# The modulation of a two-layer transformer block with its weight tiles turned: VectorE sums each row, and four slabs share the first block of inputs

## The reference, cut to what matters

```python
c_act = jax.nn.silu(c)
mod = c_act @ w_ada[l] + b_ada[l]          # w_ada[l] is 2048 x 12288
shift_a, scale_a, gate_a, shift_m, scale_m, gate_m = jnp.split(mod, 6)
h = rms_norm(x, g_pre_mix[l]) * (1.0 + scale_a) + shift_a
y = token_mixer(h, ...)                    # h @ w_in, mLSTM and attention, @ w_out
x = x + gate_a * rms_norm(y, g_post_mix[l])
h = rms_norm(x, g_pre_mlp[l]) * (1.0 + scale_m) + shift_m
y = squared_relu_mlp(h, w_up[l], w_down[l])
x = x + gate_m * rms_norm(y, g_post_mlp[l])
```

## Time and profile before

| what | value |
|---|---|
| median of 3 runs | 3728.34 us (3727.72 to 3730.37) |
| the profiled execution's own time | 3729.29 us |
| its span | 3727.5 us |
| PE busy | 3394.7 us, 91% |
| DVE busy | 2639.3 us, 71% |
| ACT busy | 1569.2 us, 42% |
| mean granted TensorE clock | 0.929 of full |

### The profile page before, as it was taken

How to read it: one execution, slowest core, us unless ns; L and a number is a source line. 1 busy time by engine, 2 the same in 40 slices (tenths; PEclk the granted TensorE clock), 3 DMA queues, 4 the chain that set the end, 5 groups by cost and what they waited for, 6 DMA issues and landing times.

```text
span 3727.5 us, 46843 instructions
## 1 busy us (share of the span) xinstructions
PE 3394.7 (91%) x18574; PEld 2861.8 (77%) x18574; DVE 2639.3 (71%) x4213; ACT 1569.2 (42%) x2160; POOL 0.2 (0%) x4
## 2 busy tenths in 40 slices
PE   1888889999999988889889999998988999899997
PEld 1676777888888867778678888886877588688886
DVE  7878777777777778777776655567499665656665
ACT  1444554343434454444434444445333054534343
POOL 0000000000000000000000000000000000000000
PEclk6788899999999988989899999998859999899999
DMA  9756576777777745456466555554405045354353
GB/s 397 290 212 226 218 267 223 273 259 275 256 279 257 268 168 223 178 192 254 182 238 236 186 188 191 191 186 158 177 28 200 13 166 207 125 190 151 123 181 113
DMA packets 111304, 759.09 MB, mean 204 GB/s; under 512 B 13936, under 2 KB 18288, under 8 KB 21104
## 3 DMA queue, kind: packets, MB, share of 16 engines
q1 hardware_dynamic: 107936, 749.72, 55.5%
q10 hardware_dynamic: 3152, 6.38, 0.5%
HBM read 747.58 MB, written 8.39 MB: 203 GB/s over the span
## 4 chain that ended last, share of the span: by engine, by line
PE 65%; DVE 21%; ACT 7%; issue 3%; ACTq 0%; DMA 0%; DVEq 0%; SPq 0%
PE bk L301 64%; DVE wl L1196 7%; ACT wh L691 5%; DVE acc L1204 4%; DVE sq L1204 2%; DVE pr L1196 1%; ACT L691 1%; DVE X L1196 1%; PE bk L305 1%; DVE ss L1196 1%; DVE Hst L1196 1%; DVE hb L1196 1%; DVE HX L1204 1%; DVE sm L1380 0%; DVE co L1204 0%
## 5 line engine op out<-in xcount | busy, mean ns | idle before, releaser
L1196 DVE TENSOR_TENSOR wl<-raw,wh 128x2048 fp32r<-128x2048 f32 x507 | 1161.2, 2290 | 439.7 <-ACT wh L691 439.0
L301 PE MATMUL bk<-HX,wh 128*128 128x512 f32 x5040 | 1288.6, 406 | 59.8 <-ACT HX L691 32.0
L301 PEld LDWEIGHTS bk<-HX,wh 128*128 128x128 f32 x5040 | 952.8, 194 | 301.6 <-issue 67.9
L691 ACT ACTIVATE wh<-raw 128x2048 fp32r<-128x2048 f32 x507 | 966.9, 1907 | 72.5 <-DMA raw<-in_w_in 72.4
L301 PEld LDWEIGHTS bk<-HX,wl 128*128 128x128 f32 x5040 | 654.0, 194 | 34.8 <-DVE wl L1196 10.9
L301 PE MATMUL bk<-HX,wl 128*128 128x256 f32 x5040 | 662.3, 285 | 6.9 <-DVE wl L1196 6.8
L301 PE MATMUL bk<-hb,wh 128*128 128x512 f32 x2048 | 495.0, 393 | 15.1 <-ACT hb L691 6.0
L301 PEld LDWEIGHTS bk<-hb,wh 128*128 128x128 f32 x2048 | 378.1, 189 | 96.6 <-issue 13.4
L1204 DVE SCALAR_TENSOR_TENSOR acc<-raw,sm,acc 128x2048 f32<-128x2048 f32 x180 | 423.2, 2351 | 21.2 <-DMA raw<-in_w_ada 1.1
L301 PEld LDWEIGHTS bk<-hb,wl 128*128 128x128 f32 x2048 | 266.1, 194 | 9.8
L301 PE MATMUL bk<-hb,wl 128*128 128x256 f32 x2048 | 269.5, 285 | 0.0
(11 more groups left out here) (259 smaller groups left out, 2914.5 us busy)
## 6 DMA issues: line engine op xcount, KB each, us to landing
raw<-in_w_ada SPq DMA_DIRECT2D x192, 1024.0 KB, 4.9
raw<-in_w_up SPq DMA_DIRECT2D x128, 1024.0 KB, 4.8
raw<-in_w_down SPq DMA_DIRECT2D x128, 1024.0 KB, 4.8
raw<-in_w_in SPq DMA_DIRECT2D x74, 1024.0 KB, 4.9
raw<-in_kv_w SPq DMA_DIRECT2D x33, 1024.0 KB, 4.8
raw<-in_w_out SPq DMA_DIRECT2D x32, 1024.0 KB, 5.3
raw<-in_s_w_in SPq DMA_DIRECT2D x32, 1024.0 KB, 4.9
raw<-in_fox_w_in SPq DMA_DIRECT2D x32, 1024.0 KB, 4.8
```

Source lines behind the costliest of these rows:

```text
L301: return e.matmul(o_, l_, r_, start=start, stop=stop, skip_group_check=True)
L691: return e.activation(o_, i_, f, **kw)
L1196: return e.tensor_tensor(o_, a_, b_, op)
```

## The change

The modulation's tiles are stored the other way round: 128 outputs on the partitions and all 2048 inputs along the row. `CB` holds silu(c), twice as large, the same in every partition; it is made once from a new 1 MB input `c_row` by a Tanh on ACT and one operation of DVE. One scalar_tensor_tensor per tile then multiplies the tile by CB and by 0.5, writes the product back over the tile in RAW, and its accumulator writes the row sums: 128 finished outputs, one column of `MOD`. `ACC`, `ROW`, PE's sums, ACT's row copies, the 40 small DMAs, and the wait of each tile for the one before are gone.

The two first pieces come in turns, tile k of the scale and tile k of the shift, and every four pairs are finished into four blocks of h. Slabs 0 to 3 are loaded and split between these tiles, into WH and WL places of their own (1 to 4) and banks 0 to 3. `ramp` multiplies them side by side, block by block of h, and starts when all four are split. The constants (`cst`) are loaded behind the first five tiles instead of first. The other 160 tiles are spread anew: behind slabs 4 to 51, one each; 80 behind MLP0's slabs (64 before); 16 behind the last slab of IN1 and the first 15 of OUT1 (32 in IN1 and OUT1 before, 25 of them in IN1); 16 in MLP1.

```diff
-def spread(first, last):
-    return [first + (last - first) * i // 15 for i in range(16)]
-AFTER = ([[-1] * 16, [-1] * 16]
-         + [spread(0, 13), spread(16, 31), spread(34, 47)]
-         + [spread(J_MLP[0] + 32 * p, J_MLP[0] + 32 * p + 28) for p in range(4)]
-         + [spread(J_IN[1] + 3, J_IN[1] + 22), spread(J_IN[1] + 25, J_IN[1] + 46)]
-         + [spread(J_MLP[1] + 2, J_MLP[1] + 30)])
-SUM_AFTER = {14: 2, 32: 3, 49: 4, J_IN[1] + 23: 9, J_IN[1] + 48: 10, J_MLP[1] + 32: 11}
-SUM_AFTER.update({J_MLP[0] + 32 * p + 30: 5 + p for p in range(4)})
+RAMP = 4
+def spread(first, last, n):
+    return [first + (last - first) * i // (n - 1) for i in range(n)]
+AFTER = (spread(4, 51, 48) + spread(J_MLP[0], J_MLP[0] + 124, 80) + spread(J_OUT[1] - 1, J_OUT[1] + 14, 16)
+         + spread(J_MLP[1] + 2, J_MLP[1] + 32, 16))
...
+for _k in range(16):
+    _tile_next(_k)
+    _tile_next(16 + _k)
+    if _k % 3 == 2 and _k // 3 < RAMP:
+        _slab_next(_k // 3)
+for _j in range(RAMP, N_SLABS):
+    _slab_next(_j)
...
+BANK_OF = [j if j < RAMP else j % 3 for j in range(N_SLABS)]
+PLACE_OF = [j + 1 if j < RAMP else j % 2 for j in range(N_SLABS)]
...
                 return first
-            def sums(j):
-                if j not in SUM_AFTER:
-                    return
-                p = SUM_AFTER[j]
-                e.wait_ge(s_free, TILE_POS[16 * p + 15] + 1)
-                bank = claim(3)
-                for c in range(4):
-                    last = mm(bank[32 * c:32 * c + 1, :], ONES[:, 0:1], ACC[:, 512 * c:512 * c + 512], True, True)
-                last.then_inc(s_sum, 1)
-                release[3] = (s_sumr, p - 1)
+            def ramp(j0, count, x, first):
+                e.wait_ge(s_hi, j0 + count)
+                e.wait_ge(s_free, POS[j0 + count - 1] + 1)
+                banks = [claim(BANK_OF[j0 + r]) for r in range(count)]
+                for k in range(KT):
+                    first(k)
+                    for r in range(count):
+                        w = PLACE_OF[j0 + r]
+                        mm(banks[r][:, :], WH[w][:, k, :], x(k).rearrange("p a t -> p (a t)"), k == 0, False)
+                        last = mm(banks[r][:, 0:T], WL[w][:, k, :], x(k)[:, 0, :], False, k == KT - 1)
+                last.then_inc(s_slab, count)
+                release[3] = (s_ev, j0 + count)
             def x_sum(i):
...
             def layer(l):
+                if l == 0:
+                    ramp(0, RAMP, hx, h_ready(0))
                 for n in range(N_IN):
-                    slab(J_IN[l] + n, hx, None if n else h_ready(2 * l))
+                    if l or n >= RAMP:
+                        slab(J_IN[l] + n, hx, None if n else h_ready(2 * l))
...
-            for p in range(2):
-                bank = claim(4 + p)
-                e.wait_ge(s_free, TILE_POS[16 * p + 15] + 1)
-                for k in range(KT):
-                    last = mm(bank[:, k:k + 1], ACC[:, k::16], ONES[:, 0:1], True, True)
-                last.then_inc(s_sum, 1)
-                release[4 + p] = (s_mod, p + 1)
...
-                if j >= 2:
-                    e.wait_ge(s_slab, j - 1)
-                act(WH[j % 2][:, :, :], RAW[POS[j] % RING][:, :, :], ACT.Copy).then_inc(s_hi, 1)
+                if before(j, PLACE_OF) >= 0:
+                    e.wait_ge(s_slab, before(j, PLACE_OF) + 1)
+                act(WH[PLACE_OF[j]][:, :, :], RAW[POS[j] % RING][:, :, :], ACT.Copy).then_inc(s_hi, 1)
...
-            def sums(j):
-                if j - 1 not in SUM_AFTER:
-                    return
-                p = SUM_AFTER[j - 1]
-                l, piece = PIECES[p]
-                e.wait_ge(s_sum, p + 1)
-                if p > 2:
-                    e.wait_ge(s_row, 64 * (p - 2))
-                for c in range(4):
-                    last = act(ROW[32 * c:32 * c + 1, :], BK[3][32 * c:32 * c + 1, :], ACT.Copy)
-                last.then_inc(s_sumr, 1)
-                e.wait_ge(s_sumr, p - 1)
-                for c in range(4):
-                    e.dma_start(MOD[32 * c:32 * c + 32, 6 * l + piece, :],
-                                ROW[32 * c:32 * c + 1, :].rearrange("o (p k) -> o p k", k=16)).then_inc(s_row, 16)
...
             def layer(l):
-                for n in range(N_IN):
-                    if n:
+                for n in range(0 if l else RAMP, N_IN):
+                    if l == 0 and n == RAMP:
+                        for i in range(RAMP):
+                            mixer_half(l, i)
...
             e.wait_ge(s_x, 16)
+            e.wait_ge(s_cb0, 1)
             x_rms(0)
-            high(0)
-            for l in range(2):
-                to_h(2 * l, MOD[:, 6 * l + SHIFT_A, :])
-                layer(l)
+            for k in range(KT):
+                if k % 4 == 0:
+                    for j in ((0,), (1,), (2, 3), ())[k // 4]:
+                        high(j)
+                to_h_block(0, k, MOD[:, SHIFT_A, :])
...
-                ada(j)
-            def ada(j):
-                for t in TILES_AFTER.get(j, []):
-                    p, k = divmod(t, 16)
-                    place = TILE_POS[t]
-                    raw = RAW[place % RING][:, :, :].rearrange("p a b -> p (a b)")
-                    e.wait_ge(s_raw[place % RING], 16 * (place // RING + 1))
-                    if k == 0:
-                        if p:
-                            e.wait_ge(s_sum, p)
-                        ts(ACC[:, :], raw, CA[:, 0:1], None, ALU.mult).then_inc(s_free, 1)
-                    else:
-                        e.wait_ge(s_free, place)
-                        stt(ACC[:, :], raw, CA[:, k:k + 1], ACC[:, :], ALU.mult, ALU.add).then_inc(s_free, 1)
...
+                if j >= RAMP:
+                    for t in TILES_AFTER.get(j, []):
+                        tile(t)
+            def tile(t):
+                p, k = divmod(t, 16)
                 l, piece = PIECES[p]
-                col_ = MOD[:, 6 * l + piece, :]
+                place = TILE_POS[t]
+                raw = RAW[place % RING][:, :, :].rearrange("p a b -> p (a b)")
+                e.wait_ge(s_raw[place % RING], 16 * (place // RING + 1))
+                stt(raw, raw, 0.5, CB[:, :], ALU.mult, ALU.mult, MOD[:, 6 * l + piece, k:k + 1]).then_inc(s_free, 1)
+                if p > 1 and k == 15:
+                    e.wait_ge(s_free, place + 1)
+                    ended(p, slice(0, 16)).then_inc(s_mod, 1)
...
-            def sums(j):
-                if j - 3 in SUM_AFTER:
-                    p = SUM_AFTER[j - 3]
-                    l, piece = PIECES[p]
-                    e.wait_ge(s_row, 64 * (p - 1))
-                    piece_ended(p, MOD[:, 6 * l + piece, :])
...
-            ccol = PRM[:, C_COL:C_COL + 16]
+            e.wait_ge(s_ct0, 1)
+            stt(CB[:, :], SQ[:, 0:8, :].rearrange("p k t -> p (k t)"), 1.0, CB[:, :], ALU.add,
+                ALU.mult).then_inc(s_cb0, 1)
+            e.wait_ge(s_cb0, 1)
             e.wait_ge(s_prm, 16)
-            e.wait_ge(s_ce, 1)
-            settled(ts(CE, CE, 1.0, None, ALU.add))
-            settled(e.reciprocal(CE, CE))
-            tt(CA, CE, ccol, ALU.mult).then_inc(s_ca, 1)
-            e.wait_ge(s_ca, 1)
             e.wait_ge(s_cst, 16)
-            ada(-1)
-            low(0)
-            for p in range(2):
-                e.wait_ge(s_sum, p + 1)
-                piece_ended(p, BK[4 + p][:, 0:16])
-            for l in range(2):
-                gs, sh = modulation(l, SCALE_A), modulation(l, SHIFT_A)
-                to_h(2 * l, gs, sh)
-                layer(l)
+            gs, sh = MOD[:, SCALE_A, :], MOD[:, SHIFT_A, :]
+            for k in range(KT):
+                tile(k)
+                tile(16 + k)
+                if k % 3 == 2 and k // 3 < RAMP:
+                    low(k // 3)
+                if k % 4 == 3:
+                    q = slice(k - 3, k + 1)
+                    e.wait_ge(s_free, TILE_POS[16 + k] + 1)
+                    ended(0, q)
+                    settled(ended(1, q))
+                    if k == 3:
+                        e.wait_ge(s_rx, 1)
+                    for i in range(k - 3, k + 1):
+                        scaled(0, i, gs)
+                    for i in range(k - 3, k + 1):
+                        h_low(0, i, sh)
+            low(RAMP)
+            layer(0)
+            gs, sh = modulation(1, SCALE_A), modulation(1, SHIFT_A)
+            to_h(2, gs, sh)
+            layer(1)
             third()
             fourth()
...
-            e.dma_start(CST[:, :], d["cst"]).then_inc(s_cst, 16)
+            e.dma_start(CB[:, :], d["c_row"]).then_inc(s_c, 16)
             e.dma_start(PRM[:, :], d["prm"]).then_inc(s_prm, 16)
-            for j in range(-1, N_SLABS):
-                others(j)
-                if j >= 0:
-                    load(POS[j], source(j))
-                for t in TILES_AFTER.get(j, []):
-                    (l, piece), k = PIECES[t // 16], t % 16
-                    load(TILE_POS[t], d["w_ada"][l, piece, k])
```

(92 more changed lines are left out.)

52 lines of the change are left out of this document (23 added, 29 removed).

## The result

The changed kernel takes 3669.72 us (median, 3665.61 to 3671.2), the one before 3729.07 beside it (3727.72 to 3730.37): a ratio of 0.9839, interval 0.9822 to 0.9856. So it is faster by 59 us. The forecast was 3695 with a range of 3674 to 3720: the right side, and a time outside the range. The profiled execution of the changed kernel took 3671.2 us, with a span of 3669.4.

The account below looks back on a forecast made before the run. No single bound: PE in MLP stages without tiles, waits between PE and DVE in the mixers, DVE at the start. Terms -7 + 0 - 1 + 4 - 25 - 1 - 3 = -33 gave 3696, predicted 3695 us, range 3674 to 3720.

Parts of the forecast that it names:

- IN1: -25: Stage IN1: 25 tiles leave and one comes in, saving 25 us, the largest term.
- The chain gave 33: IN1's chain of waits: 13 whole tiles, 30.6 us, with the sum's 2.4 make 33, taken to bound the gain.
- the comparison of IN0 and IN1: IN0, with more tiles and sums, took only 4.5 us more than IN1: some 0.5 us a tile, 12 in all.
- The catching up: In IN1, PE idle for 43.5 us and below full clock was said to have room to catch up.
- my second rival: IN1 and start: fewer waits keep PE at full clock; IN1 gives 33, the start 10, total 3683 or so; chance 0.12.
- The tile: 2.36: Every new tile on DVE: 2.351 less 0.09 overlap plus 0.1 for writing out the accumulator; ends 2.26 and 2.46 us.
- The start: -7: Before slab 4: DVE bounds after the constants at 25.7; slab 4 at 136.4 instead of 143.4; ends -10 and +3.
- MLP0: +4: Stage MLP0: three more tiles on the path +7.4, 35 tiles at 0.1 less -3.5; ends -6 and +8.
- MLP1: -3: Stage MLP1: 7 tiles in late up slabs instead of 8 (-2.5), and 7 x 0.1; ends -5 and 0.
- IN0 and the OUT stages: IN0: more tiles offset by cheaper ones and fewer sums, 0; OUT0 and OUT1: tiles free, sums gone, -1 us each.
- The rivals on the slow side: Every tile: writing out the accumulator is dear (chance 0.05, 3750 us), or the tile runs at half speed (0.03, about 3970).
- The halved throughput: Every tile: two non-bf16 sources with row sums run at half throughput, about 4.6 us a tile, about 3970 total; chance 0.03.

Follow-up runs that it names:

- the two last runs in IN1: Two kernels with most MLP tiles in down slabs, plus tiles back in IN1: 14 on its chain of waits, 3646.83 us; 11 off it, 3613.8 us.
- n_pointer: The changed kernel with the factor 0.5 read from a column in SBUF instead of a constant in the instruction: 3674.54 us, run once.
- n_down: The changed kernel with most tiles of MLP0 and MLP1 moved from the up slabs into the down slabs: 3619.89 us, ratio 0.9708.
- n_off_chain: The kernel of n_down with 11 tiles back in IN1, behind slabs where the chain of waits passed no tile: 3613.8 us, run once.
- n_best: n_off_chain with the constants loaded ahead of the first tile instead of behind the fifth: 3606.24 us, ratio 0.9674.
- n_best2: n_best with IN0's 33 tiles moved off that stage's chain of waits, several behind one slab: 3588.29 us, ratio 0.9627.

## Why the prediction was right or wrong

**IN1: -25, measured -34.8; this step failed.** The chain gave 33, and I took 25 because the comparison of IN0 and IN1 made a tile worth 0.5 us, and because idle PE would catch up. The comparison was wrong: it counted tiles, and the two last runs in IN1 show that a count says nothing. There 14 in the wrong places cost 30 us, and 11 in others about one. The catching up was half right. The chain's 13 tiles were 30.6 us, and PE's idle time fell by 21.1 only. What the "bound" left out was the clock: 62 us at half clock became 28, and PE's busy time fell by 11.3 more than the sum's 2.4. That the bound of 33 came so close to 34.8 is therefore partly luck: less of the tiles' time came off than it says, and the clock made up for it. The clock stood in the earlier trace rows at 0.90, and my second rival named this mechanism with 0.12; it came about, though the clock rose to 0.95 and not to full. Its 3683 was still too high, as it had the start at -10 and a tile at 2.36.

**The tile: 2.36, measured 2.21; this term was mis-sized, and its ends too.** The lower end of 2.26 took 2.351 for the instruction. The pointer factor was in the row (`sm` among the sources), but I gave it no price; `n_pointer` puts it at 0.061. The read-out, for which I put 0.1, is not on the path: it overlaps the next instruction. At the start (32 tiles), in MLP0 (35) and in MLP1 (7) 0.15 less is 11 us. Of the 25 us between the sum's -33 and the -58 of the spans, IN1 holds 10, and these three stages hold the other 15.

**The start: -7, measured -12.5.** The steps held: the wait for the constants (25.5 for 25.7), then DVE as the bound. Of the 5.5 us that the forecast was too late, 4.2 are there at the last h already (122.0 for 126.2), and 32 tiles at 0.15 are 4.8. The rest is in the last four blocks, of which only part ran at half clock (6.8 us), and in the step to slab 4. The end of -10 was too near.

**MLP0: +4, measured -2.6; MLP1: -3, measured -5.8.** The three more tiles in MLP0 and the 35 cheaper ones both counted as said; 35 x 0.25 = 8.8 of gain stood against 7, where I had 3.5. MLP1's 7 tiles give 1.8 by the price and the one that left 2.46; 1.5 us I can't place. A full price for every tile fits here because DVE is behind PE with so many of them in the late up slabs. I did not see that it has a floor: `n_down` shows that few enough tiles cost nothing there.

**IN0 and the OUT stages** came as forecast (-0.3, -0.1, -1.2 for 0, -1, -1). That IN0's two more tiles and its cheaper ones cancelled is my reading; no run separates them.

**The rivals on the slow side** fell with the first row of the tile. The halved throughput (the Trainium skill, Vector Engine (DVE) Microarchitecture Reference, Points that are easy to get wrong) does not hold here: two fp32 sources in SBUF with the accumulator written out take 2.284 us, as long as a plain tensor_tensor of the size, 2.29.

**The range** of 3674 to 3720 failed by 4 us. Its lower end allowed the sum 21 us more. The price of a tile enters the start, MLP0 and MLP1 alike, so a cheaper tile makes these stages better at once and their errors (15 us) don't cancel; IN1's 10 us came on top.

## What to carry to other kernels

Price work that is moved off a chain of waits by the pieces of it that the chain passes, not by a stage's total divided by the number of pieces. Their full length came out within 2 us in IN1 (14 tiles at 2.21 are 30.9; measured 29.8 and 30.1), but 12 us of that was PE's slower clock and 18 its idle time, so the clock is not to be added on top. In IN0 the same price for 14 tiles gave 23.2. Before moving filler work out of a stage, try other places within it: the same 33 tiles behind other slabs of IN0 saved 23 us in that stage. In a stage that PE bounds, filler is free up to PE's pace, so spread it thinly, one in three up slabs here, instead of one behind nearly each.

## What the hardware did that was not expected

- DVE's read of its accumulator takes 0.082 us and starts with the instruction behind it, so it adds nothing to the path: tiles follow each other at 2.21.
- A wait for DVE's own instruction before costs 0.19 us (2.40 against 2.21), although that instruction ends only 0.07 behind the point where the next could start.
- A factor read from a column of SBUF in place of a constant costs 0.06 us in a 128x2048 fp32 scalar_tensor_tensor (2.345 against 2.284).
- DVE's tiles in the wrong slabs slow TensorE beyond the waits: the same matmuls of IN1 took 252 us at a mean clock of 0.90 and 240 at 0.95.
- The clock also moved the stage with every tile of it in place: IN1 took 259.1 us at 0.96 in `n_off_chain` and in `n_best`, and 264.0 at 0.94 in `n_best2`, with 23.6 to 23.7 us of idle PE in all three.
